# A hybrid decoder layer on one core: smaller descriptor scratch, final gain loaded ahead, twelve diagonals and one dot column per slot, the last two row gathers and the last norm in halves

## The chip, the cores and the metric

The kernel runs on one core of one Trainium2 chip. The metric is the device time of one execution in microseconds (us). Times quoted from the trace are microseconds from the start of the profiled span.

## What is computed

One decoder layer over 256 tokens of width 1024, in float32: a mixer with two groups of attention heads, a cross-attention to 256 memory tokens, a PEER feed-forward part, and a final RMSNorm. The change touches the last two:

```python
def peer_ffn(h, w_query, sub_keys_1, sub_keys_2, expert_down, expert_up):
    # per token: 8 heads, each picks the 16 best of 128 x 128 experts
    ...
    eidx = jnp.take_along_axis(cand_idx, pos, axis=-1)
    g = jax.nn.softmax(top_s, axis=-1)
    u = expert_down[eidx]
    a = jax.nn.gelu(jnp.einsum('cd,chkd->chk', xc, u), approximate=False)
    vv = expert_up[eidx]
    return jnp.einsum('chk,chkd->cd', g * a, vv)
...
x = x + peer_ffn(rmsnorm(x, norm_ffn), ...)
return rmsnorm(x, norm_final)     # y * rsqrt(mean(y*y) + eps) * norm_final
```

For each token 8 x 16 = 128 experts are picked. Of each one a row of `expert_down` (1024 numbers) is dotted with the normed token, and a row of `expert_up` is added to the token's sum with the weight gate x gelu(dot).

## The kernel before, in words

The 256 tokens are two tiles of 128 tokens, one token per partition. Up to about 237 us the kernel does the mixer, the memory attention of tile 0 and the first head's key search. From there to the end it runs the PEER part: 256 **slots**, numbered n, 128 for each tile (16 for each of 8 heads H). The two tables lie side by side in DRAM, so that one gathered row is 8 KB (down half, then up half). One slot is:

- POOL (loop in the `gpsimd` block, L597): an indirect DMA fetches for each of the 128 tokens its row into a buffer of [128, 2048], 1 MB in all. It first waits until TensorE has used up the buffer's former content (`up_used`). The buffers form a ring of 6, later 8, 10 and, from slot 100, 12 (`RINGS`).
- DVE (`dot`, L1169): multiplies the down half with the normed token and sums into a column of `dots`, when the rows are there (`row_in`).
- ACT (`weight`, L770, L774, L779): gelu of the dot, times the gate, and a 128 x 128 diagonal matrix of it in `diag`.
- PE (`up`, L1480): diagonal x up half, two matmuls of 512 columns, accumulated in PSUM (`y` for tile 0, `v_bank` for tile 1). `h_psum` and `a_bank` hold the normed tokens.

`NS = 6` columns of `dots` and diagonals exist. So DVE also waits in slot n for the gelu of slot n-6, and ACT waits before the diagonal for PE's slot n-6. Between the slots, at places written out by hand (`slots`, `top_at`), stand the rest of tile 1's layer and the key search of the next heads on DVE (`top_part`). That search ends in the expert numbers (`IDX`, parts "ones", "picks", "experts") for which POOL waits at each head. The part "ones" and the part "picks" are two instructions of 128 x 256 each.

The final norm (`root` on ACT, `finish` on DVE) is done for tile 0 after slot 134 and for tile 1 after the last slot. ACT squares and sums the row from PSUM and takes the root, DVE takes the reciprocal and multiplies row, root and gain in one instruction (L1181), SP writes 512 KB to DRAM (L565). The gain `gfin` (a row of 4 KB, broadcast to 128 partitions, 512 KB) lies in a weight slot that `w_xo` uses before. So SP issues its load (L561) only after a wait on tile 1's product with `w_xo`.

SP issues the loads of weights in program order (L504, L558, L561). The program's descriptor scratch for POOL's DMAs has its default size.

Of the kernel before, what the change touches and what calls it, by code (L numbers as in the profile page):

```python
# [17 lines left out]
P = 128  # L18
D = 1024
SEQ = 256  # L20
T = SEQ // P
# [14 lines left out]
NS = 6  # L36
# [27 lines left out]
def hybrid_layer(nc, A, out, bias_scratch):  # L64
# [200 lines left out]
    with ctx:  # L265
# [78 lines left out]
        GATE = sb("gates", [P, 3, PK])  # L344

        dots = sb("dots", [P, NS])
# [3 lines left out]
        sums_r = diag_r.rearrange("p (a b) x -> p a (b x)", a=3)  # L350
        small, small_r = diag[0:NH, :, :].rearrange("p (a b) x -> p a (b x)", a=3), sums_r[0:NH, :, :]
# [23 lines left out]
        gfin = W[:, wslot("w_xo", 0), 0:D]  # L375
# [59 lines left out]
        out_ready, out_done = sem("out_ready"), sem("out_done")  # L435

# [21 lines left out]
        roots += [("root_y", 0, 0), ("root_y", 1, 0)]  # L458
# [9 lines left out]
        def col(name, t, i):  # L468
            return {"root_m": i, "root_h": 2 + t, "o_root": 4 + 2 * t + i, "root_x": 8 + 2 * t,
                    "root_p": 9 + 2 * t, "root_y": 12 + t}[name]  # L470
# [3 lines left out]
        ROWS += [W[:, wslot("w_xo", 1), 2 * D * i:2 * D * (i + 1)] for i in range(2)]  # L474

# [16 lines left out]
        def _(sp):  # L492
# [70 lines left out]
            for t in range(T):  # L563
                sp.wait_ge(out_ready, t + 1)
                sp.dma_start(out[0, t * P:(t + 1) * P, :], YS[t]).then_inc(out_done, 16)  # L565
# [4 lines left out]
        def _(pool):  # L570
# [13 lines left out]
            pool.memset(diag_r[:, :, :].bitcast(f32), 0.0).then_inc(sums_zero, 1)  # L584
            pool.iota(iota16[:], [[1, PK]], base=0, channel_multiplier=0,
                      allow_small_or_imprecise_dtypes=True).then_inc(io_ready, 1)
            for n in range(T * SPT):
# [7 lines left out]
                elif buffer(n) in FREED_BY:  # L595
                    pool.wait_ge(*full(FREED_BY[buffer(n)]))
                pool.indirect_dma_start(ROWS[buffer(n)], None, expert_rows,  # L597
                                        bass.IndirectOffsetOnAxis(ap=IDX[:, H % 3, k:k + 1], axis=0))\
                    .then_inc(row_in[buffer(n)], 16)
# [3 lines left out]
        def _(act):  # L603
# [162 lines left out]
            def weight(n):  # L766
# [3 lines left out]
                nc.scalar.activation(gel[:, i:i + 1], dots[:, i:i + 1], ACT.Gelu, scale=rms("root_p", n // SPT)).then_inc(gelu_done, 1)  # L770
# [25 lines left out]
            act.wait_ge(up_used, T * SPT)  # L796
            root(("root_y", 1, 0), YP[1][:, :], HTpage[1], D)
# [3 lines left out]
        def _(dve):  # L801
# [284 lines left out]
            def top_part(part, H):  # L1086
# [48 lines left out]
                elif part == "ones":  # L1135
                    after(top_mark["pairs"])
                    for s in range(2):
                        top_mark[part] = t_mark(nc.vector.tensor_tensor(
                            hot[:, s, :, :], pabf[:, s, :].unsqueeze(2).broadcast_to([P, PK, PK]),
                            iota16[:, :].unsqueeze(1).broadcast_to([P, PK, PK]), ALU.is_equal))  # L1140
                elif part == "picks":
                    after(top_mark["ones"])
                    for s in range(2):
                        top_mark[part] = t_mark(nc.vector.tensor_tensor(
                            hot[:, s, :, :], hot[:, s, :, :],
                            kf[:, s, :].unsqueeze(1).broadcast_to([P, PK, PK]), ALU.mult))
                elif part == "experts":
                    after(top_mark["picks"])
                    after(t_mark(nc.vector.tensor_reduce(picked[:, :, :], hot[:, :, :, :], AX.X, ALU.add)))
                    nc.vector.scalar_tensor_tensor(out=IDX[:, H3, :], in0=picked[:, 0, :], scalar=float(NKEY),  # L1150
# [12 lines left out]
            def dot(n):  # L1163

                i, rows = n % NS, ROWS[buffer(n)][:, 0:D]
# [23 lines left out]
            for n in range(T * SPT):  # L1189
# [14 lines left out]
                if n == SPT + NS:  # L1204
                    finish(0, YP[0][:, :])
            finish(1, YP[1][:, :])


        assert buffer(SIDE_END) == 0 and RING % NS == 0
# [331 lines left out]
```

## Time and profile before

| what | value |
|---|---|
| time, median of 3 runs (lowest, highest) | 906.3 us (903.89, 907.79) |
| time of the profiled execution | 904.22 us |
| its span, first to last instruction | 902.4 us |
| PE, DVE, ACT, POOL busy | 796.0, 561.9, 433.6, 242.8 us |
| moved by POOL's queue (q0) | 268.45 MB in 36,864 packets |
| mean granted TensorE clock | 0.985 |

The profiled execution's time is its span and 1.8 us that lie around it. Busy times add up what each engine does, whatever the others do meanwhile. What sets the end is read from the chain of waits and from the stretches in which one resource never pauses.

### The profile page before, as it was taken

The numbers are of one execution on the slowest core, as the hardware profiler recorded it, in microseconds if no ns is written. First come the engines' busy times: TensorE is split into PE (matmuls) and PEld (weight loads), VectorE is DVE, ScalarE is ACT, GpSimd is POOL, SyncE is SP. The second block draws the span as 40 slices with busy tenths as digits, with TensorE's granted clock in tenths as the row PEclk, the third lists the DMA queues.
The fourth block names the chain that finished last, engine by engine and source line by source line (L and its number), as shares of the span: only waits on it lengthen the run. The fifth ranks groups of instructions, "written<-read, shape, count | busy, mean of one in ns | idle before, by whom it ended". The sixth has DMA issues, their size and how long they took to land.

```text
span 902.4 us, 10121 instructions
## 1 busy us (share of the span) xinstructions
PE 796.0 (88%) x3195; PEld 450.2 (50%) x3195; DVE 561.9 (62%) x1396; ACT 433.6 (48%) x1078; POOL 242.8 (27%) x268
## 2 busy tenths in 40 slices
PE   7999999999999999889898997989787877788776
PEld 7999987785455455444343552444232222222221
DVE  5555344123778767777776748787676766666443
ACT  5435555333245554667444445535355353535333
POOL 0000000000143333433343341624333333343310
PEclk9999999999999999999999899999999999999999
DMA  9898532072399999999999999999999999999993
GB/s 332 235 293 288 195 133 94 1 280 93 142 405 421 391 423 421 415 422 421 422 420 421 421 421 410 401 416 423 421 422 421 422 422 421 422 422 421 422 420 133
DMA packets 63317, 314.24 MB, mean 348 GB/s; under 512 B 7899, under 2 KB 12068, under 8 KB 30500
## 3 DMA queue, kind: packets, MB, share of 16 engines
q0 software_dynamic: 36864, 268.45, 71.9%
q1 hardware_dynamic: 25308, 43.61, 13.8%
q10 hardware_dynamic: 1096, 1.59, 1.2%
q8 instruction: 23, 0.38, 0.2%
q14 instruction: 26, 0.21, 0.1%
HBM read 311.01 MB, written 2.62 MB: 348 GB/s over the span
## 4 chain that ended last, share of the span: by engine, by line
PE 42%; DMA 38%; ACT 9%; issue 5%; DVE 5%; POOL 1%; POOLq 0%; ACTq 0%
DMA weights<-in_expert_rows,expert_idx 24%; PE y L1480 10%; DMA qkvb<-in_expert_rows,expert_idx 7%; PE v_bank L1480 7%; DMA mem_k<-in_expert_rows,expert_idx 6%; PE v_bank L1235 4%; PE a_bank L1245 4%; PE h_psum L1235 4%; PE v_bank L1245 3%; PE a_bank L1235 3%; PE h_psum L1245 3%; ACT diag L779 1%; ACT L770 1%; ACT L762 1%; ACT spare_r L676 1%
## 5 line engine op out<-in xcount | busy, mean ns | idle before, releaser
L597 POOL DMA_INDIRECT weights<-in_expert_rows,expert_idx x172 | 161.4, 939 | 260.7 <-PE y L1480 118.1
L770 ACT ACTIVATE gelu<-dots,stat 128x1 f32<-128x1 f32 x256 | 75.3, 294 | 307.0 <-DVE dots L1169 300.6
L1480 PE MATMUL v_bank<-weights,diag 128*128 128x512 f32 x344 | 169.9, 623 | 39.8 <-ACT diag L779 39.8
L1480 PE MATMUL y<-weights,diag 128*128 128x512 f32 x344 | 161.7, 606 | 17.7 <-ACT diag L779 17.5
L1169 DVE CUSTOM_DVE_ANT_0 weights<-a_bank,weights 128x1024 f32<-128x1024 f32 x86 | 105.3, 1224 | 74.9 <-DMA weights<-in_expert_rows,expert_idx 74.8
L1169 DVE CUSTOM_DVE_ANT_0 weights<-h_psum,weights 128x1024 f32<-128x1024 f32 x86 | 105.1, 1223 | 54.7 <-DMA weights<-in_expert_rows,expert_idx 52.6
L597 POOL DMA_INDIRECT qkvb<-in_expert_rows,expert_idx x54 | 51.0, 944 | 316.6 <-DVE expert_idx L1026 234.6
L1480 PEld LDWEIGHTS v_bank<-weights,diag 128*128 128x128 f32 x344 | 61.1, 193 | 144.7 <-ACT diag L779 94.0
L1480 PEld LDWEIGHTS y<-weights,diag 128*128 128x128 f32 x344 | 62.4, 191 | 98.2 <-issue 56.9
L779 ACT ACTIVATE diag<-ident,wgt 128x128 f32<-128x128 f32 x256 | 102.8, 402 | 8.4
L774 ACT ACTIVATE wgt<-gelu,gates 128x1 f32<-128x1 f32 x256 | 75.4, 295 | 8.3
L1480 PE MATMUL y<-qkvb,diag 128*128 128x512 f32 x136 | 66.5, 617 | 7.6 <-ACT diag L779 7.6
L889 DVE TENSOR_TENSOR weights_r<-weights,spare_r 128x2048 fp32r<-128x2048 f32 x19 | 43.5, 2291 | 36.9 <-ACT spare_r L676 36.9
L1169 DVE CUSTOM_DVE_ANT_0 qkvb<-h_psum,qkvb 128x1024 f32<-128x1024 f32 x34 | 41.6, 1223 | 22.1 <-DMA qkvb<-in_expert_rows,expert_idx 21.9
L1480 PE MATMUL v_bank<-qkvb,diag 128*128 128x512 f32 x80 | 40.4, 630 | 11.5 <-ACT diag L779 11.5
L676 ACT CAST spare_r<-weights 128x2048 fp32r<-128x2048 f32 x19 | 36.0, 1897 | 19.1 <-PE v_bank L1245 14.6
L1480 PEld LDWEIGHTS y<-qkvb,diag 128*128 128x128 f32 x136 | 24.6, 194 | 39.6 <-issue 21.0
L1245 PE MATMUL h_psum<-weights_r 128*128 128x256 f32 x128 | 36.2, 282 | 0.0
L1169 DVE CUSTOM_DVE_ANT_0 qkvb<-a_bank,qkvb 128x1024 f32<-128x1024 f32 x20 | 24.5, 1225 | 15.5 <-DMA qkvb<-in_expert_rows,expert_idx 15.5
L1480 PEld LDWEIGHTS v_bank<-qkvb,diag 128*128 128x128 f32 x80 | 13.9, 191 | 36.3 <-ACT diag L779 25.8
L1235 PE MATMUL v_bank<-weights,scaled_gffn 128*128 128x512 f32 x64 | 29.2, 595 | 0.6 <-issue 0.6
L1480 PE MATMUL v_bank<-mem_v,diag 128*128 128x512 f32 x44 | 21.7, 616 | 6.2 <-ACT diag L779 6.2
(288 smaller groups left out, 1281.7 us busy)
## 6 DMA issues: line engine op xcount, KB each, us to landing
weights<-in_w_in SPq DMA_DIRECT2D x5, 2048.0 KB, 32.3
weights<-in_w_xk SPq DMA_DIRECT2D x2, 2048.0 KB, 16.6
weights<-in_w_xv SPq DMA_DIRECT2D x2, 2048.0 KB, 10.7
weights<-in_w_out SPq DMA_DIRECT2D x2, 2048.0 KB, 8.8
weights<-in_w_xq SPq DMA_DIRECT2D x2, 2048.0 KB, 7.9
weights<-in_w_xo SPq DMA_DIRECT2D x2, 2048.0 KB, 11.1
weights<-in_expert_rows,expert_idx POOLq DMA_INDIRECT x172
weights<-in_w_in SPq DMA_DIRECT2D x2, 1024.0 KB, 8.5
```

The costliest lines, as they stand in the source:

```text
L597: pool.indirect_dma_start(ROWS[buffer(n)], None, expert_rows, bass.IndirectOffsetOnAxis(ap=IDX[:, H % 3, k:k + 1], axis=0))\
L676: act.copy(WH_r[t % 2], half_block(t, W)).then_inc(high_ready, 1)
L762: nc.scalar.activation(texp[:], tv[:], ACT.Exp, bias=tneg[:, 0:1], scale=rms("root_p", H // PH), accum_out=tsum[:, 0:1])\
L770: nc.scalar.activation(gel[:, i:i + 1], dots[:, i:i + 1], ACT.Gelu, scale=rms("root_p", n // SPT)).then_inc(gelu_done, 1)
L774: nc.scalar.activation(wgt[:, i:i + 1], gel[:, i:i + 1], ACT.Copy, scale=GATE[:, H % 3, k:k + 1])\
L779: nc.scalar.activation(diag[:, i, :], ident[:, :], ACT.Copy, scale=wgt[:, i:i + 1])\
L889: nc.vector.tensor_tensor(half_block(t, W_r), half_block(t, W), WH_r[t % 2].bitcast(f32), ALU.subtract).then_inc(low_ready, 1)
L1169: nc.vector.tensor_tensor_reduce(out=rows, in0=HP[n // SPT][:, :], in1=rows, scale=1.0, scalar=0.0, op0=ALU.mult, op1=ALU.add, accum_out=d ...
L1235: ins = nc.tensor.matmul(bank[:, lo:lo + n], lhs(k), rhs(k), start=(k == 0), stop=(k == chunks - 1))
L1245: ins = nc.tensor.matmul(bank[:, lo:lo + n], a(k), b(k), start=(k == 0 and p == 0), stop=(k == KC - 1 and p == 2))
L1480: ins = nc.tensor.matmul(YP[t][:, b * BLK:(b + 1) * BLK], diag[:, i, :], ROWS[r][:, D + b * BLK:D + (b + 1) * BLK], start=False, stop=last)
```

## The change

Six things are changed.

1. The descriptor scratch is given as 4,096 bytes a partition in place of the default.
2. `gfin` gets a tile of its own, and SP issues its load right behind the last weight load, with no wait.
3. `dots` has a column for each of the 256 slots, `gel`, `wgt` and `diag` have twelve. DVE's wait for the gelu of slot n-6 and ACT's wait for PE's slot n-6 are gone, with no new one in their place.
4. "ones" and "picks" are one instruction of 128 x 512 each.
5. The last two slots (254, 255) are gathered as half rows, in the order down 254, down 255, up 254, up 255, of 512 KB each. The table is seen as rows of 4 KB for this; DVE computes the half rows' numbers (`last_idx`) with the last head's expert numbers.
6. Slot 255 has no diagonal and no matmul. DVE adds up half x weight to PE's sum in two halves of 512 columns. ACT squares each half, DVE multiplies each by the gain meanwhile, and the row is scaled by the root's reciprocal, half on ACT and half on DVE. PE's matmuls of slot 254 report each half.

```diff
-NS = 6
+NS = 12
+DMA_SCRATCH = 4096
...
-        dots = sb("dots", [P, NS])
+        dots = sb("dots", [P, T * SPT])
...
-        gfin = W[:, wslot("w_xo", 0), 0:D]
+        gfin = sb("gfin", [P, D])[:, :]
...
-            sp.wait_ge(v_full, VN[("xo", 1, 0)] + 1)
             sp.dma_start(gfin, A["norm_final"].rearrange("(a d) -> a d", a=1).broadcast_to([P, D]))\
...
+                if n < LAST - 1:
...
+                else:
+                    i = n - (LAST - 1)
+                    pool.indirect_dma_start(ROWS[buffer(n)][:, 0:D], None, half_rows,
+                                            bass.IndirectOffsetOnAxis(ap=last_idx[:, i:i + 1], axis=0))\
+                        .then_inc(row_in[buffer(n)], 16)
+            for i in range(2):
+                pool.indirect_dma_start(ROWS[buffer(LAST - 1 + i)][:, D:2 * D], None, half_rows,
+                                        bass.IndirectOffsetOnAxis(ap=last_idx[:, 2 + i:3 + i], axis=0)).then_inc(up_in[i], 16)
...
+                if n == LAST:
+                    return
                 act.wait_ge(w_done, n + 1)
-                if n >= NS:
-                    act.wait_ge(up_used, n - NS + 1)
...
             nc.scalar.activation(stat[:, 15:16], eps[:, 0:1], ACT.Sqrt)
-            act.wait_ge(up_used, T * SPT)
-            root(("root_y", 1, 0), YP[1][:, :], HTpage[1], D)
+            for b in range(2):
+                act.wait_ge(last_sum, b + 1)
+                nc.scalar.activation(hp[:, last_half[b]], YS[1][:, last_half[b]], ACT.Square, accum_out=last_sq[b])\
+                    .then_inc(last_square, 1)
+            act.wait_ge(last_square, 2)
+            act.wait_ge(last_eps, 1)
+            nc.scalar.activation(last_sq[1], last_sq[1], ACT.Sqrt, bias=last_sq[0], scale=1.0 / D).then_inc(sq_done, 1)
+            act.wait_ge(last_root, 1)
+            act.wait_ge(last_gain, 1)
+            nc.scalar.activation(YS[1][:, last_half[0]], last_gained[:, last_half[0]], ACT.Copy, scale=last_sq[1])\
+                .then_inc(last_ready, 1)
...
-                if n >= NS:
-                    dve.wait_ge(gelu_done, n - NS + 1)
...
+            def finish_last():
+                i = LAST % NS
+                dve.wait_ge(w_done, LAST + 1)
+                dve.wait_ge(up_in[1], 16)
+                for b in range(2):
+                    dve.wait_ge(half_used, b + 1)
+                    nc.vector.scalar_tensor_tensor(out=YS[1][:, last_half[b]],
+                                                   in0=ROWS[buffer(LAST)][:, D + b * BLK:D + (b + 1) * BLK],
+                                                   scalar=wgt[:, i:i + 1], in1=YP[1][:, last_half[b]],
+                                                   op0=ALU.mult, op1=ALU.add).then_inc(last_sum, 1)
...
+            pe.wait_ge(diag_done, LAST)
+            pe.wait_ge(up_in[0], 16)
+            for b in range(2):
+                nc.tensor.matmul(YP[1][:, b * BLK:(b + 1) * BLK], diag[:, (LAST - 1) % NS, :],
+                                 ROWS[buffer(LAST - 1)][:, D + b * BLK:D + (b + 1) * BLK], start=False, stop=True)\
+                    .then_inc(half_used, 1)
...
-    nc = bacc.Bacc("TRN2", target_bir_lowering=False, num_devices=1)
+    nc = bacc.Bacc("TRN2", target_bir_lowering=False, num_devices=1, dynamic_dma_scratch_size=DMA_SCRATCH)
```

DVE at the end of the program, before (`ISA ...dots` is the dot, the `ISA dots` row behind it reads its sum):

```order
L1169 ISA mem_v,dots<-a_bank,mem_v 128x1024 [waits gelu_done,row_in9]
L1169 ISA dots 128x1
L1169 ISA weights,dots<-a_bank,weights 128x1024 [waits gelu_done,row_in10]
L1169 ISA dots 128x1
L1169 ISA weights,dots<-a_bank,weights 128x1024 [waits gelu_done,row_in11]
L1169 ISA dots 128x1
L820 RECIPROCAL stat<-stat 128x1 [waits sq_done]
L1181 SCALAR_TENSOR_TENSOR x_and_h<-v_bank,stat,weights 128x1024 [waits ld_gfin,dve_ch]
```

The same place with the change:

```order
L1204 ISA weights,dots<-a_bank,weights 128x1024 [waits row_in11]
L1204 ISA dots 128x1
L1224 SCALAR_TENSOR_TENSOR x_and_h<-weights,wgt,v_bank 128x512 [waits half_used,up_in1,w_done]
L1224 SCALAR_TENSOR_TENSOR x_and_h<-weights,wgt,v_bank 128x512 [waits half_used]
L1229 TENSOR_TENSOR x_and_h<-x_and_h,gfin 128x512 [waits last_sum]
L1232 TENSOR_SCALAR stat<-stat 128x1 [waits last_square]
L1233 TENSOR_TENSOR x_and_h<-x_and_h,gfin 128x512
L1236 RECIPROCAL stat<-stat 128x1 [waits sq_done]
L1239 TENSOR_SCALAR x_and_h<-x_and_h,stat 128x512 [waits last_gain,last_root]
```

Two instructions behind the last dot have become seven, of half the width.

DVE inside the slots, where a head's key search ends, before:

```order
L1138 TENSOR_TENSOR one_hot<-pos_ab_f,iota 128x256 [waits top_ch]
L1138 TENSOR_TENSOR one_hot<-pos_ab_f,iota 128x256
L1169 ISA weights,dots<-a_bank,weights 128x1024 [waits gelu_done,row_in11]
L1169 ISA dots 128x1
L1144 TENSOR_TENSOR one_hot<-one_hot,key_idx_f 128x256 [waits top_ch]
L1144 TENSOR_TENSOR one_hot<-one_hot,key_idx_f 128x256
L1169 ISA qkvb,dots<-a_bank,qkvb 128x1024 [waits gelu_done,row_in0]
```

And with the change:

```order
L1168 TENSOR_TENSOR one_hot<-pos_ab_f,iota 128x512 [waits top_ch]
L1204 ISA weights,dots<-a_bank,weights 128x1024 [waits row_in11]
L1204 ISA dots 128x1
L1173 TENSOR_TENSOR one_hot<-one_hot,key_idx_f 128x512 [waits top_ch]
L1204 ISA qkvb,dots<-a_bank,qkvb 128x1024 [waits row_in0]
```

Each dot now waits for one semaphore in place of two. An instruction that waits for a second semaphore has an instruction that only waits in front of it, which these rows don't show. In the program as built, DVE has 1,569 instructions before, 297 of which only wait, and 1,299 with the change, 49 of which only wait. ACT has 1,350 (333 only wait) before, and 1,103 (85) with the change. PE, POOL and SP differ by two at most.

## Rows read from the trace of the kernel before

**Rows 1.** Page, part 2 (GB/s in 40 slices of 22.6 us) and part 3 (queue: packets, MB, share)
```profile
GB/s 332 235 293 288 195 133 94 1 280 93 142 405 421 391 423 421 415 422 421 422 420 421 421 421 410 401 416 423 421 422 421 422 422 421 422 422 421 422 420 133
...
q0 software_dynamic: 36864, 268.45, 71.9%
```

**Rows 2.** Waits from 250 to 902 us: who waited for whom, total us, times, longest
```profile
DVE weights L1169 <- DMA weights<-in_expert_rows,expert_idx: 127.5, 145, 2.0
```

**Rows 3.** Timeline of DVE: the dot of slot 225 (start us, us, engine, line, operation)
```profile
817.50 1.23 DVE L1169 CUSTOM_DVE_ANT_0 weights<-a_bank,weights 128x1024 f32<-128x1024 f32 x1 [1.67 <-DMA weights<-in_expert_rows,expert_idx]
```

**Rows 4.** Busy time in a stretch: PE, PEld, DVE, ACT, POOL, clock, DMA share, GB/s
```profile
885.00:892.00 7.00, 5.55 (x13) 1.81 (x11) 3.33 (x6) 2.97 (x9) 0.00 (x0) 1.00 0.12 50
```

**Rows 5.** Timeline from the dot of slot 255 to the last store, 892 to 900 us
```profile
892.01 1.22 DVE L1169 CUSTOM_DVE_ANT_0 weights<-a_bank,weights 128x1024 f32<-128x1024 f32 x1 [1.23 <-DMA weights<-in_expert_rows,expert_idx]
...
893.93 0.40 ACT L779 ACTIVATE diag<-ident,wgt 128x128 f32<-128x128 f32 x1
894.35 1.28 ACT L795 ACT_TABLE_LOAD   x1
...
894.38 1.98 PE L1480 MATMUL v_bank<-weights,diag 128*128 128x512 f32 x4 [0.47 <-ACT diag L779]
...
895.64 0.20 ACT L795 ACTIVATE stat<-eps 128x1 f32<-128x1 f32 x1
896.40 1.02 ACT L614 ACTIVATE x_and_h<-v_bank 128x1024 f32<-128x1024 f32 x1 [0.56 <-PE v_bank L1480]
...
897.55 0.29 ACT L627 ACTIVATE stat<-stat,eps 128x1 f32<-128x1 f32 x1
897.88 0.16 DVE L820 RECIPROCAL stat<-stat 128x1 f32<-128x1 f32 x1 [4.64 <-ACT stat L627]
898.08 1.28 DVE L1181 SCALAR_TENSOR_TENSOR x_and_h<-v_bank,stat,weights 128x1024 f32<-128x1024 f32 x1
899.39 0.34 SPq L565 DMA_DIRECT2D out<-x_and_h  x1
```

**Rows 6.** Groups by form: tiles, shapes, count, busy us, mean ns, idle before
```profile
L875 DVE TENSOR_TENSOR x_and_h_r<-x_and_h,scaled_gffn_r 128x512 fp32r<-128x512 f32 x4 | 2.6, 683 | 0.0
L614 ACT ACTIVATE qkvb<-x_and_h 128x512 f32<-128x512 f32 x4 | 2.5, 626 | 6.5 <-DVE x_and_h L951 6.5
L959 DVE TENSOR_SCALAR x_and_h<-x_and_h,stat 128x512 f32<-128x512 f32 x4 | 1.9, 486 | 0.1
```

**Rows 7.** Timeline of POOL: the gathers of slots 113 and 255
```profile
512.25 0.94 POOL L597 DMA_INDIRECT qkvb<-in_expert_rows,expert_idx  x1 [0.53 <-issue]
...
866.92 0.94 POOL L597 DMA_INDIRECT weights<-in_expert_rows,expert_idx  x1 [1.55 <-PE v_bank L1480]
```

**Rows 8.** Timeline: the load of the gain on SP, and the dots of slots 88, 90, 91
```profile
465.30 0.34 SPq L561 DMA_DIRECT2D weights<-in_norm_final  x1
...
468.03 1.22 DVE L1169 CUSTOM_DVE_ANT_0 mem_k<-h_psum,mem_k 128x1024 f32<-128x1024 f32 x1 [0.72 <-DMA mem_k<-in_expert_rows,expert_idx]
...
474.27 1.22 DVE L1169 CUSTOM_DVE_ANT_0 qkvb<-h_psum,qkvb 128x1024 f32<-128x1024 f32 x1 [1.34 <-DMA qkvb<-in_expert_rows,expert_idx]
477.70 1.22 DVE L1169 CUSTOM_DVE_ANT_0 qkvb<-h_psum,qkvb 128x1024 f32<-128x1024 f32 x1 [1.67 <-DMA qkvb<-in_expert_rows,expert_idx]
```

**Rows 9.** DMA queues from 468 to 474 us: packets, MB, share of 16 engines
```profile
q1 hardware_dynamic: 143, 0.52, 21.8%
```

**Rows 10.** The page's group of the diagonals: busy us, mean ns, idle before
```profile
L779 ACT ACTIVATE diag<-ident,wgt 128x128 f32<-128x128 f32 x256 | 102.8, 402 | 8.4
```

**Rows 11.** Timeline: the dots of slots 177 and 178
```profile
695.41 1.23 DVE L1169 CUSTOM_DVE_ANT_0 weights<-a_bank,weights 128x1024 f32<-128x1024 f32 x1 [0.73 <-DMA weights<-in_expert_rows,expert_idx]
698.79 1.23 DVE L1169 CUSTOM_DVE_ANT_0 weights<-a_bank,weights 128x1024 f32<-128x1024 f32 x1 [1.77 <-DMA weights<-in_expert_rows,expert_idx]
```

**Rows 12.** DMA queues from 696 to 698 us
```profile
q14 instruction: 1, 0.01, 1.0%
```

**Rows 13.** Timeline: the gather of slot 25 on POOL and its dot on DVE
```profile
301.82 0.98 POOL L597 DMA_INDIRECT qkvb<-in_expert_rows,expert_idx  x1 [2.57 <-PE y L1480]
...
309.57 1.23 DVE L1169 CUSTOM_DVE_ANT_0 qkvb<-h_psum,qkvb 128x1024 f32<-128x1024 f32 x1 [2.37 <-DMA qkvb<-in_expert_rows,expert_idx]
```

More of the change, by code:

```diff
@@ L435, in hybrid_layer @@
         out_ready, out_done = sem("out_ready"), sem("out_done")
+        up_in, half_used = [sem(f"up_in{i}") for i in range(2)], sem("half_used")
+        last_sum, last_square, last_eps, last_gain = sem("last_sum"), sem("last_square"), sem("last_eps"), sem("last_gain")
+        last_root, last_ready = sem("last_root"), sem("last_ready")
         def bank_of(key):
@@ L474, in hybrid_layer @@
         ROWS += [W[:, wslot("w_xo", 1), 2 * D * i:2 * D * (i + 1)] for i in range(2)]
+        LAST = T * SPT - 1
+        last_sq = [stat[:, 13 + b:14 + b] for b in range(2)]
+        last_half = [slice(b * BLK, (b + 1) * BLK) for b in range(2)]
+        last_gained = HTpage[1]
         def rms(name, t):
@@ L559, in _ @@
                              [:, :, b * BLK:(b + 1) * BLK]).then_inc(ld_query[b], 16)
-            sp.wait_ge(v_full, VN[("xo", 1, 0)] + 1)
             sp.dma_start(gfin, A["norm_final"].rearrange("(a d) -> a d", a=1).broadcast_to([P, D]))\
                 .then_inc(ld_gfin, 16)
-            for t in range(T):
-                sp.wait_ge(out_ready, t + 1)
-                sp.dma_start(out[0, t * P:(t + 1) * P, :], YS[t]).then_inc(out_done, 16)
+            sp.wait_ge(out_ready, 1)
+            sp.dma_start(out[0, 0:P, :], YS[0]).then_inc(out_done, 16)
+            sp.wait_ge(last_ready, 2)
+            sp.dma_start(out[0, P:2 * P, :], YS[1]).then_inc(out_done, 16)
             sp.wait_ge(out_done, 16 * T)
@@ L1136, in top_part @@
                     after(top_mark["pairs"])
[L1137 to L1140, printed above, removed]
+                    top_mark[part] = t_mark(nc.vector.tensor_tensor(
+                        hot[:, :, :, :], pabf[:, :, :].unsqueeze(3).broadcast_to([P, 2, PK, PK]),
+                        iota16[:, :].unsqueeze(1).unsqueeze(1).broadcast_to([P, 2, PK, PK]), ALU.is_equal))
                 elif part == "picks":
                     after(top_mark["ones"])
[L1143 to L1146, printed above, removed]
+                    top_mark[part] = t_mark(nc.vector.tensor_tensor(
+                        hot[:, :, :, :], hot[:, :, :, :],
+                        kf[:, :, :].unsqueeze(2).broadcast_to([P, 2, PK, PK]), ALU.mult))
                 elif part == "experts":
@@ L1149, in top_part @@
                     after(t_mark(nc.vector.tensor_reduce(picked[:, :, :], hot[:, :, :, :], AX.X, ALU.add)))
+                    if H == T * PH - 1:
+                        after(t_mark(nc.vector.scalar_tensor_tensor(
+                            out=last_expert[:, :], in0=picked[:, 0, PK - 2:PK], scalar=float(NKEY),
+                            in1=picked[:, 1, PK - 2:PK], op0=ALU.mult, op1=ALU.add)))
+                        for half in range(2):
+                            t_mark(nc.vector.tensor_scalar(last_idx[:, 2 * half:2 * half + 2], last_expert[:, :], 2.0,
+                                                           float(half), ALU.mult, ALU.add))
                     nc.vector.scalar_tensor_tensor(out=IDX[:, H3, :], in0=picked[:, 0, :], scalar=float(NKEY),
@@ L1203, in _ @@
                     top_part(part, H)
[L1204 to L1206 removed]
+                if n == SPT + 6:
+                    finish_first()
+            finish_last()
         assert buffer(SIDE_END) == 0 and RING % NS == 0
```

45 lines of the change are left out of this document (30 added, 15 removed).

## The prediction

> **What bounds the kernel now.** I read the page first. Its GB/s slices stand at 420 or near it from slice 12 to 39, and POOL's queue has moved 268.45 MB [rows 1]. So the slot part is one long gather. The waits say the same: DVE stood 127.5 us in 145 waits for rows of the weight buffers alone [rows 2], and no engine is waited for on the way to a landing. The timeline gives the beat. The dot of slot 225 starts at 817.50 [rows 3], that of slot 255 at 892.01 [rows 5], both straight behind their landing: 74.51 us for 30 slots, 2.484 us each.
>
> The beat is not the mean engine's. From 885 to 892 us the DMA engines move only 50 GB/s [rows 4], 350 KB in all, while slots 253 to 255 still land one beat apart. So most DMA engines have finished, and one or two last ones (64 KB per slot in 2.484 us is 26.4 GB/s each) set every landing. What is put into or taken out of their work after slot 25 therefore shows at the end one to one. A pause of POOL that does not outlast the backlog shows nowhere.
>
> Behind the last landing comes a chain of its own [rows 5]: dot 892.01, diagonal 893.93, matmuls 894.38 to 896.36, square 896.40, root 897.55, reciprocal 897.88, product 898.08, store issued 899.39, end of the span 902.4. That is 10.4 us, 7.4 of them up to the store's issue. The change can work in two places, the DMA engines' queue and this chain.
>
> **The end of the program.** Let L be the landing of the last rows, 892.01 now. With halves in the order down, down, up, up, each half beat is 1.24 us, so the down half of slot 255 lands at L-2.48, the up half of 254 at L-1.24. I walk the engines.
> - ACT: the diagonal starts 1.92 us behind the start of a dot [rows 5]. For 254 it ends at L-3.73+1.92+0.40 = L-1.4. For 255 the weight is ready near L-0.6; then the table load (1.28) and the dummy root run from about L-0.5 to L+1.0, where the table load now lies under the matmuls.
> - PE: 1.98 us for both halves of a slot [rows 5], 0.99 each. It starts at L-1.24 and gives the halves at L-0.25 and L+0.75.
> - DVE: a 128x512 operation of two tensors takes 0.68 us [rows 6]. First sum L to L+0.7, second L+0.8 to L+1.5, first product with the gain to L+2.2, the small eps step, second product to L+3.0.
> - ACT: square of 512 columns 0.63 us [rows 6] and some 0.15 for the read of its sum: L+1.0 to L+1.8, then to L+2.55. Root (0.29) to L+2.9, covered by DVE's second product.
> - Reciprocal (0.16) to L+3.2, then a half on DVE (0.49) and one on ACT (about 0.6, by the square's row) side by side: L+3.9.
>
> The store is issued at L+3.9 in place of L+7.4, and what follows it stays 3.0 us. **Gain 3.5 us.** DVE's order is the limit. If the handshakes cost 0.1 us more at each of eight steps it is 2.7; if the squares start earlier than I have them, up to 4.2.
>
> The two extra gathers of POOL cost nothing: slot 255's gather is issued at 866.92 [rows 7] and lands 25.1 us later, ten beats of backlog against two more issues of 1.24 us. No other queue stands behind them. DVE gets three small instructions for the halves' numbers in the last key search, some 0.6 us of a DVE that waits over 1 us per beat, long before the end.
>
> What a half gather costs the DMA engines I take from the only 512 KB transfer with 4 KB rows amid the gathers, the gain's (next part): 1.27 us, against 1.24 for half a beat. So four halves cost 4 x 1.27 in place of 2 x 2.484, 0.1 us more. The upper bound is 0.6 us, if 4 KB rows ran as the load in the next part at its worst.
>
> The Trainium skill speaks against this step ("DMA: Bandwidth & Descriptors", "Anatomy of one DMA"): it gives each transfer of POOL's path about 2.0 us fixed and bytes over 436 GB/s, and its rule is to batch to 1 MiB or more. As an estimate from that page, two more transfers would cost 4 us if they ran one behind the other. The trace shows a 1 MB slot each 2.484 us, less than the 4.4 us of that formula, so the fixed part overlaps here.
>
> **The gain's load.** SP issues it at 465.30, in the middle of the gathers [rows 8], and 0.52 MB pass on its queue from 468 to 474 us [rows 9]. From slot 88 to slot 90 the dots take 6.24 us for two beats (4.97): 1.27 us late, a half beat's worth. With the change the load is issued right behind the query load at about 212 us, where the slices show 93 and 142 GB/s [rows 1], before the first gather. The same bytes go where nothing waits. **Gain 1.27 us**; bounds 0 (if the beat were PE's there) and 2.2 (if the next late slot were its doing too). What comes after is one unbroken backlog, so nothing takes it back.
>
> **The waits.** ACT stood idle 8.4 us before all 256 diagonals [rows 10], 0.033 each, the bare handshake. DVE's waits in the dots are for rows. Neither of the two removed waits ever held anything, and twelve diagonals in place of six free nothing. The one-instruction "ones" and "picks" save about 0.15 us per head on DVE, which waits for rows anyway. As waits, all of it is worth zero.
>
> As instructions it may not be. Slot 178's dot starts 3.38 us behind slot 177's [rows 11], 0.9 over the beat, and 2 us earlier the instruction queue moved a packet [rows 12]. I found that step of 0.9 us before slots 91, 118, 154, 178, 201 and 225, each with a packet of that queue in the 2 to 4 us before; other packets of it had no effect. Between the four last of these the built program has 115, 114 and 114 DVE instructions, and 13 more by the rows that a search splits into two: 128 each time. So DVE's own instruction stream is fetched over one of the late DMA engines, 128 instructions at a time. Slot 25 to 255 has 582.4 us [rows 13, 5], 571.3 by the beat. Of the 11.1 over it 1.27 is the gain's load, as much again tile 0's store, and the rest is nine steps of 0.93. With the change DVE has 1,012 instructions there against 1,263, so 7.9 fetches in place of 9.9. **Gain 1.9 us**, bounds 0 (the steps have another cause) and 2.8 (one more fetch falls out).
>
> **Sum.** 3.5 + 1.27 + 1.9 - 0.1 = 6.6 us. The profiled execution goes from 904.2 to 897.6, its span from 902.4 to 895.8. The median before is 906.3, 2.1 above the profiled one, so against it I expect 899.7.
>
> **Rivals.**
> - *The instruction steps stay.* The steps of 0.9 us come from something periodic and not from DVE's fetches. For it: 8 KB at 26.4 GB/s are 0.3 us, a third of the step. Against it: the count of 128 holds three times. Then 904.2 - 4.7, or 901.6 against the median, about at the edge of what counts as faster.
> - *The tail gives less.* The handshakes between three engines, or the halves landing later, leave 1 to 1.5 us of 3.5, and one fetch falls badly. Sum 3 us: 903.3.
> - *The scratch throttles POOL (slower).* POOL must find room in the scratch for its descriptors. Each slot has 144 packets (36,864 by 256 [rows 1]), 9 per DMA engine, and a smaller scratch is reused more often. If POOL let its transfers drain at such a point, the next slot would land no sooner than 7.75 us after its issue, as slot 25 did with a near empty queue (301.82 to 309.57 [rows 13]), 5.3 us beyond the beat. The trace doesn't tell how often that would be. One drain in 32 slots is eight, 42 us: 942 against the median. Two drains already eat the forecast's gain, and it begins where fewer than about three slots can be in flight. Against it: POOL's gathers take 0.94 us at slot 113 as at slot 255, with 0.53 us idle before the one and a wait for PE before the other [rows 7], so the scratch of before shows no such point in mid stream.
>
> By the Trainium skill ("SBUF — State Buffer", "SBUF size: 192, 224, or 256?" and "DMA: Bandwidth & Descriptors", "The descriptor swizzle") the default scratch is 16 KiB and a 1 MiB transfer takes 9 descriptors per engine and side, at 16 B each. As an estimate 4 KiB then hold 28 transfers against 10 in flight, and no throttle follows. No run so far shows the smaller size.
>
> **How the numbers follow.** A measurement of this kernel can tell about 0.5% from no change, 4.5 us, so "faster" is below 901.8 us. The forecast has 0.50, the staying steps 0.24, the small tail 0.18, the throttle 0.05; 0.03 is for what I don't see. The forecast with its bounds is faster nearly always, the second case about half the time, the third rarely: faster 0.64, within 0.5% 0.29, slower 0.07. The range takes the sum's own ends (2.5 to 9 us off the median) and the 2 us by which single executions differ: 895.5 to 904.8. It leaves out the throttle.
>
> **What would show it.** The store's issue 3.9 us behind the last landing, and 6.9 from there to the end of the span (a longer chain: the tail rival). The gain's load before 225 us, and no late slots at 89 and 90. The 0.9 us steps 28 to 30 slots apart in the last hundred slots, in place of 24 (if still 24: the first rival). The beat unchanged at 2.484 us; a longer beat, or POOL idle with free buffers and no engine to wait for, would be the throttle and would prove me wrong. DVE and ACT busy times should hardly differ.

## The result and the profile after

| | before | changed |
|---|---|---|
| time, median (lowest, highest), 7 runs each | 905.09 us (903.89, 908.65) | 897.94 us (897.27, 901.68) |
| ratio, 95% interval | | 0.9918 [0.9903, 0.9933] |
| profiled execution, its span | 904.22, 902.4 us | 897.27, 895.5 us |

The kernel is 0.8% faster: 7.1 us by the medians, 6.9 by the spans of the two profiled executions. The forecast was 899.7 (897.6 for a profiled execution), range 895.5 to 904.8.

The page of the changed kernel, parts 2 and 3:

```profile
GB/s 333 233 287 303 178 152 94 1 282 118 112 407 422 393 424 420 411 421 421 422 420 423 421 421 422 412 422 422 420 422 422 422 421 422 422 421 421 422 422 201
...
q0 software_dynamic: 37152, 268.45, 72.4%
```

The bytes of POOL's queue are the same, with 288 packets more (two transfers of 144) than in [rows 1]. The slices stand at the same 420.

The timeline of the changed kernel answers to [rows 8]. The gain's load is now issued at 212 us, and the dots of slots 88 to 91 stand one beat apart:

```profile
212.29 0.58 SPq L573 DMA_DIRECT2D gfin<-in_norm_final  x1
...
467.14 1.22 DVE L1204 CUSTOM_DVE_ANT_0 mem_k<-h_psum,mem_k 128x1024 f32<-128x1024 f32 x1 [0.72 <-DMA mem_k<-in_expert_rows,expert_idx]
469.61 1.22 DVE L1204 CUSTOM_DVE_ANT_0 mem_v<-h_psum,mem_v 128x1024 f32<-128x1024 f32 x1
472.10 1.23 DVE L1204 CUSTOM_DVE_ANT_0 qkvb<-h_psum,qkvb 128x1024 f32<-128x1024 f32 x1 [0.86 <-DMA qkvb<-in_expert_rows,expert_idx]
474.58 1.23 DVE L1204 CUSTOM_DVE_ANT_0 qkvb<-h_psum,qkvb 128x1024 f32<-128x1024 f32 x1 [0.71 <-DMA qkvb<-in_expert_rows,expert_idx]
```

Two beats take 4.96 us, where they took 6.24.

A late slot is one whose dot starts 0.9 us or more over the beat behind the dot before it, as slot 178 does in [rows 11]. Before, they were 91, 118, 154, 178, 201 and 225. Now they are 109, 160, 190 and 220, two fewer, and the last three stand thirty apart. (Slots 101 and 135 are late in every kernel, by 2.8 and 4.5 us. They are left out here.) Here are slots 189 and 190 of the changed kernel:

```profile
722.32 1.23 DVE L1204 CUSTOM_DVE_ANT_0 weights<-a_bank,weights 128x1024 f32<-128x1024 f32 x1 [0.91 <-DMA weights<-in_expert_rows,expert_idx]
...
725.78 1.23 DVE L1204 CUSTOM_DVE_ANT_0 weights<-a_bank,weights 128x1024 f32<-128x1024 f32 x1 [1.82 <-DMA weights<-in_expert_rows,expert_idx]
```

3.46 us, 0.98 over the beat.

The end of the changed kernel, from the dot of slot 253 on, answers to [rows 5]:

```profile
883.35 1.22 DVE L1204 CUSTOM_DVE_ANT_0 mem_v<-a_bank,mem_v 128x1024 f32<-128x1024 f32 x1 [1.23 <-DMA mem_v<-in_expert_rows,expert_idx]
...
884.59 1.22 DVE L1204 CUSTOM_DVE_ANT_0 weights<-a_bank,weights 128x1024 f32<-128x1024 f32 x1
...
885.72 1.98 PE L1538 MATMUL v_bank<-mem_v,diag 128*128 128x512 f32 x4 [0.47 <-ACT diag L801]
...
885.84 1.23 DVE L1204 CUSTOM_DVE_ANT_0 weights<-a_bank,weights 128x1024 f32<-128x1024 f32 x1
...
887.54 1.88 PE L1577 MATMUL v_bank<-weights,diag 128*128 128x512 f32 x4
...
887.74 1.28 ACT L817 ACT_TABLE_LOAD   x1
...
888.71 1.50 DVE L1224 SCALAR_TENSOR_TENSOR x_and_h<-weights,wgt,v_bank 128x512 f32<-128x512 f32 x2 [1.64 <-PE v_bank L1577]
...
889.49 0.60 ACT L820 ACTIVATE h_psum<-x_and_h 128x512 f32<-128x512 f32 x1 [0.25 <-DVE x_and_h L1224]
...
890.24 0.69 DVE L1229 TENSOR_TENSOR x_and_h<-x_and_h,gfin 128x512 f32<-128x512 f32 x1
...
890.91 0.68 DVE L1233 TENSOR_TENSOR x_and_h<-x_and_h,gfin 128x512 f32<-128x512 f32 x1
891.09 0.29 ACT L824 ACTIVATE stat<-stat 128x1 f32<-128x1 f32 x1
891.51 0.15 DVE L1236 RECIPROCAL stat<-stat 128x1 f32<-128x1 f32 x1
891.70 0.72 ACT L827 ACTIVATE x_and_h<-x_and_h,stat 128x512 f32<-128x512 f32 x1 [0.32 <-DVE stat L1236]
891.70 0.48 DVE L1239 TENSOR_SCALAR x_and_h<-x_and_h,stat 128x512 f32<-128x512 f32 x1
892.45 0.34 SPq L578 DMA_DIRECT2D out<-x_and_h  x1
```

The down halves of slots 254 and 255 follow slot 253 at half beats (1.24, 1.25 us). The table load lies under the matmuls and the root under DVE's second product. From the dot of slot 253 to the store's issue it is now 9.10 us; before it was 12.30 (887.09 to 899.39). To the end of the span it is 12.1, before 15.3. So the end is 3.2 us shorter.

So the two profiles differ in three stretches. Up to the dot of slot 60: 397.5 and 397.0 us, 0.5 less. From slot 60 to slot 253, 193 beats of 2.4835 us: 10.25 and 7.01 us over the beat, 3.24 less. From there to the end 3.2 less. Together 6.9.

### The profile page after: what moved, and what is told of

It reads as the page before. It is cut to its first block, busy times and chain, and to the rows that moved or that the text cites. A ratio compares the mean times of both kernels' runs of the same rounds, so it can differ in the third digit from the quotient of the medians.

```text
span 895.5 us, 9600 instructions
## 1 busy us (share of the span) xinstructions
PE 788.4 (88%) x3191; PEld 447.6 (50%) x3191; DVE 561.7 (63%) x1374; ACT 433.9 (48%) x1080; POOL 247.5 (28%) x270
## 4 chain that ended last, share of the span: by engine, by line
DMA 40%; PE 40%; ACT 8%; DVE 8%; issue 3%; POOL 1%; ACTq 0%; POOLq 0%; DVEq 0%
DMA mem_v<-in_expert_rows,expert_idx 14%; DMA mem_k<-in_expert_rows,expert_idx 11%; PE y L1538 10%; DMA qkvb<-in_expert_rows,expert_idx 8%; DMA weights<-in_expert_rows,expert_idx 7%; PE v_bank L1293 4%; PE v_bank L1538 4%; PE a_bank L1303 4%; PE h_psum L1293 4%; PE v_bank L1303 3%; PE a_bank L1293 3%; PE h_psum L1303 3%; ACT diag L801 1%; DVE weights L1204 1%; DVE qkvb L1204 1%
## 5 line engine op out<-in xcount | busy, mean ns | idle before, releaser
L1538 PE MATMUL v_bank<-weights,diag 128*128 128x512 f32 x336 | 163.7, 617 | 37.4 <-ACT diag L801 37.4
L1538 PE MATMUL y<-weights,diag 128*128 128x512 f32 x344 | 158.9, 599 | 16.6 <-ACT diag L801 16.5
L1538 PEld LDWEIGHTS v_bank<-weights,diag 128*128 128x128 f32 x336 | 59.1, 191 | 138.1 <-ACT diag L801 89.7
```

Of the source, the lines that this page charges most:

```text
L1538: ins = nc.tensor.matmul(YP[t][:, b * BLK:(b + 1) * BLK], diag[:, i, :], ROWS[r][:, D + b * BLK:D + (b + 1) * BLK], start=False, stop=last)
```

## The experiments

All kernels but only_scratch are the changed kernel with something put back, added or moved, or as it is (after_again). Three numbers of each come from its trace. The span is known to 0.1 us, so the last column is good to 0.05. The ratios come from five to twelve executions each, beside the kernel before on the same chip.

| kernel | ratio to before, 95% | span | dot of slot 60 | over the beat, 60 to 253 | slot 253 to end |
|---|---|---|---|---|---|
| before | | 902.4 | 397.5 | 10.25 | 15.31 |
| changed | 0.9918 [0.9903, 0.9933] | 895.5 | 397.0 | 7.01 | 12.15 |
| dve_wait | 0.9952 [0.9934, 0.9971] | 898.3 | 397.9 | 8.96 | 12.08 |
| dve_two | 0.9941 [0.9917, 0.9965] | 898.7 | 398.5 | 8.76 | 12.11 |
| dve_three | 0.998 [0.9965, 0.9996] | 904.6 | 402.8 | 10.39 | 12.11 |
| act_wait | 0.9927 [0.9905, 0.9949] | 896.7 | 398.0 | 7.27 | 12.13 |
| gain_late | 0.9949 [0.9929, 0.9969] | 898.2 | 398.3 | 8.41 | 12.15 |
| whole_old_norm | 0.9975 [0.9955, 0.9995] | 900.9 | 399.3 | 6.89 | 15.36 |
| halves_old_norm | 0.9951 [0.9937, 0.9966] | 898.3 | 398.1 | 7.12 | 13.81 |
| store_late | 0.994 [0.9915, 0.9964] | 897.8 | 401.1 | 5.27 | 12.09 |
| store_late_again | 0.9905 [0.989, 0.9919] | 895.5 | 398.0 | 6.05 | 12.16 |
| only_scratch | 1.0002 [0.9986, 1.0018] | 903.2 | 398.9 | 9.62 | 15.31 |
| scratch_1k | 0.9924 [0.991, 0.9938] | 898.9 | 400.6 | 6.83 | 12.13 |
| after_again | 0.9921 [0.9907, 0.9936] | 900.1 | 402.2 | 6.48 | 12.07 |

The ratios of kernels that ran on different chips can't be compared as closely as the stretches. One kernel, store_late and store_late_again, has 0.994 on one chip and 0.9905 on another, 3.2 us apart at 905. The changed kernel has its ratio from the first measurement and from a chip on which only_scratch, scratch_1k and store_late_again ran as well. The other seven kernels with something put back are slower than it by their ratios (0.8 us for act_wait, 2.8 for gain_late, 3.1 for dve_wait, 5.2 for whole_old_norm, 5.6 for dve_three) by more than their last two columns say (0.26, 1.4, 1.95, 3.1, 3.4). In their traces all of them reach slot 60 later than the first profile of the changed kernel, which was early (see the part on the scatter). The prices below are those of the stretches.

### Does the number of DVE's instructions set the late slots?

The first kernel puts DVE's wait back:

```diff
                 dve.wait_ge(row_in[buffer(n)], 16 * (len(users(n)) + 1))
+                if n >= 6:
+                    dve.wait_ge(gelu_done, n - 6 + 1)
```

> The changed kernel with DVE's wait for the gelu of six slots back put into each dot again; the wait is always met, so it holds nothing, but it adds 250 DVE instructions that only wait. Theory (DVE's own instruction fetch costs one step of 0.93 us in the landings each 128 instructions): the last steps stand 24 slots apart in place of 30, about 2 steps more from slot 25 on, 1.9 us slower than the changed kernel, 899.2 in the profile. Rival (something periodic): the steps stay 30 slots apart, no difference.

The late slots are 93, 120, 158, 184, 206 and 231, two more than in the changed kernel. The last four stand 24 apart on average, and the stretch is 1.95 us longer, two steps. Slots 205 and 206 of this kernel:

```profile
764.92 1.22 DVE L1206 CUSTOM_DVE_ANT_0 mem_v<-a_bank,mem_v 128x1024 f32<-128x1024 f32 x1 [0.91 <-DMA mem_v<-in_expert_rows,expert_idx]
768.36 1.23 DVE L1206 CUSTOM_DVE_ANT_0 weights<-a_bank,weights 128x1024 f32<-128x1024 f32 x1 [1.79 <-DMA weights<-in_expert_rows,expert_idx]
```

The second puts ACT's wait back:

```diff
                 act.wait_ge(w_done, n + 1)
+                if n >= NS:
+                    act.wait_ge(up_used, n - NS + 1)
                 nc.scalar.activation(diag[:, i, :], ident[:, :], ACT.Copy, scale=wgt[:, i:i + 1])\
```

> The changed kernel with ACT's wait for PE of twelve slots back put before each diagonal again; always met, 243 ACT instructions more that only wait. Theory: the steps of 0.93 us stay at slots 160, 190 and 220 and the time stays within 0.5 us, since only DVE's fetches cost. Rival (any engine's instruction traffic costs): 2 steps more, 1.9 us slower.

The late slots stay at 109, 160, 190 and 220; the stretch is 0.26 us longer, within what two runs of one kernel differ by (7.01 and 6.48). Slots 189 and 190:

```profile
723.43 1.23 DVE L1206 CUSTOM_DVE_ANT_0 weights<-a_bank,weights 128x1024 f32<-128x1024 f32 x1 [0.92 <-DMA weights<-in_expert_rows,expert_idx]
...
726.87 1.23 DVE L1206 CUSTOM_DVE_ANT_0 weights<-a_bank,weights 128x1024 f32<-128x1024 f32 x1 [1.80 <-DMA weights<-in_expert_rows,expert_idx]
```

Two kernels with more waits in the dots followed:

> The changed kernel with two waits put into each dot again, both always met, 500 DVE instructions more. Theory: steps 19 to 20 slots apart, nearly 4 steps more than the changed kernel, 3.6 us slower, 900.9 in the profile. Rival: steps 30 slots apart, no difference.

The forecast was wrong, since the kernel isn't what it took it for: two waits share one instruction, so it has one instruction more than dve_wait in all, 1,549 against 1,548. The late slots are 158, 183, 206 and 231 again, 1.75 us more than the changed kernel. So twice the waits in the same number of instructions change nothing: it is the instructions that count. With three waits

```diff
+                if n >= 6:
+                    dve.wait_ge(gelu_done, n - 6 + 1)
+                    dve.wait_ge(w_done, n - 6 + 1)
+                    dve.wait_ge(diag_done, n - 6 + 1)
```

> The changed kernel with three waits put into each dot again, all always met. The built program has 499 DVE instructions more than the changed one (two waits share one instruction, so the kernel with two waits had only as many as the one with one). Theory: steps of 0.95 us 19 slots apart in the last hundred slots, 3 steps more from slot 60 on than the changed kernel, 3 us slower. Rival (the waits themselves, not their number, move the steps): as with one wait, 24 slots apart, 2 us slower.

DVE has 1,798 instructions, the late slots from 150 on are 154, 174, 196, 216 and 238, 21 apart where 19 were expected, and the stretch is 3.4 us over the changed kernel's. What the instruction queue moved from 236 to 880 us tells the engines apart. Row q14 of the DMA view of the kernel before, the changed one, dve_wait, dve_three and act_wait, in this order:

```profile
q14 instruction: 22, 0.18, 0.1%
```
```profile
q14 instruction: 18, 0.15, 0.1%
```
```profile
q14 instruction: 20, 0.16, 0.1%
```
```profile
q14 instruction: 22, 0.18, 0.1%
```
```profile
q14 instruction: 20, 0.16, 0.1%
```

ACT's wait and DVE's wait each bring two packets back, but only DVE's packets bring late slots. So the rival of something periodic falls, and so does "any instruction traffic". What is shown: from about slot 90 on, each 128 DVE instructions cost the landings 0.95 us, waits that are always met included, and the same packets for ACT cost nothing that can be told.

The trace's semaphore records say why the two engines differ. A gather counts its semaphore up sixteen times, and its slot can start with the last of these. From slot 150 on, the sixteenth comes 1.0 us or more behind the fifteenth in every trace that was kept, and 2.6 us in the last landing of the changed kernel. Taking each increment for the end of one part of the gather, one part in sixteen sets the beat. In act_wait a packet of the instruction queue moves at 724.48. For slot 190 the first fifteen increments then come 2.48 to 2.50 us behind those of slot 189, and only the sixteenth is late (3.44). Another packet moves at 703.98. For slot 183 only the fifteenth is late (3.17), and the sixteenth comes on the beat, 1.8 us behind it. It is the same in all fourteen traces: from slot 155 to slot 245 each late slot has its sixteenth increment late by 0.9 to 1.0 us, and the other packets delay earlier increments by 0.3 to 0.9, which nothing waits for. In act_wait and in the kernel before, these others stand 126 to 134 of ACT's recorded instructions apart, about 30 slots. In the changed kernel they stand 129 apart on average, 34 to 44 slots. So they are ACT's. DVE's packets delay the part that comes last, and ACT's one that has time.

### The gain's load

```diff
+            sp.wait_ge(v_full, VN[("xo", 1, 0)] + 1)
             sp.dma_start(gfin, A["norm_final"].rearrange("(a d) -> a d", a=1).broadcast_to([P, D]))\
```

> The changed kernel with the gain's load put back behind the wait on tile 1's product with w_xo, amid the gathers; it keeps its own tile. Theory: 0.52 MB come back into the late DMA engine's work, dots of slots 88 to 91 late by 1.27 us in all, 1.3 us slower. Rival (a beat set by PE there, or the load's 4 KB rows at half rate): 0, or 2.2 us.

Slots 88 to 91 of this kernel:

```profile
469.04 1.23 DVE L1205 CUSTOM_DVE_ANT_0 mem_k<-h_psum,mem_k 128x1024 f32<-128x1024 f32 x1 [0.72 <-DMA mem_k<-in_expert_rows,expert_idx]
472.14 1.23 DVE L1205 CUSTOM_DVE_ANT_0 mem_v<-h_psum,mem_v 128x1024 f32<-128x1024 f32 x1 [0.75 <-DMA mem_v<-in_expert_rows,expert_idx]
475.25 1.23 DVE L1205 CUSTOM_DVE_ANT_0 qkvb<-h_psum,qkvb 128x1024 f32<-128x1024 f32 x1 [1.48 <-DMA qkvb<-in_expert_rows,expert_idx]
477.74 1.23 DVE L1205 CUSTOM_DVE_ANT_0 qkvb<-h_psum,qkvb 128x1024 f32<-128x1024 f32 x1 [0.72 <-DMA qkvb<-in_expert_rows,expert_idx]
```

6.21 us for two beats, 1.25 us late, and the next slot on the beat. In the kernel before, slot 91 was late by 0.95 as well; here it is not. That confirms that this third late slot was an instruction step and not the load. The stretch is 1.4 us longer.

### The end in two parts

Two kernels undo the end. The first gathers the last two rows whole, sends slot 255 through diagonal and PE, and squares, roots and multiplies the row in one piece. The second keeps the half gathers and undoes the rest; PE waits for each up half:

```diff
-            for b in range(2):
-                act.wait_ge(last_sum, b + 1)
-                nc.scalar.activation(hp[:, last_half[b]], YS[1][:, last_half[b]], ACT.Square, accum_out=last_sq[b])\
+            act.wait_ge(up_used, T * SPT)
+            nc.scalar.activation(HTpage[1], YP[1][:, :], ACT.Square, accum_out=last_sq[0]).then_inc(last_square, 1)
...
-                nc.vector.tensor_scalar(YS[1][:, last_half[1]], last_gained[:, last_half[1]], last_sq[1], None, ALU.mult)\
+                nc.vector.scalar_tensor_tensor(out=YS[1], in0=YP[1][:, :], scalar=last_sq[0], in1=gfin,
+                                               op0=ALU.mult, op1=ALU.mult).then_inc(last_ready, 1)
...
+                if n >= LAST - 1:
+                    pe.wait_ge(up_in[n - (LAST - 1)], 16)
+                flat_up(n)
```

> The changed kernel with the last two slots gathered as whole rows, a diagonal and matmuls for slot 255 again, and the last norm in one piece as before. Theory: the chain behind the last landing is 10.4 us again in place of 7.2, 3.2 us slower than the changed kernel, the landings unchanged. Rival (the halves also cost or give something in the DMA engines): a difference other than 3.2 us, seen in the landing of the last rows.

> The changed kernel with the half gathers kept, but slot 255 through diagonal and PE, and the norm in one piece. Theory: the last landing is slot 255's up half, and only its two matmuls (1.98 us) and the norm (4.4 us up to the store's issue) stand behind it; the diagonal is ready before. So some 1.5 us slower than the changed kernel and 1.7 faster than with whole rows. Rival (the gain is all in the norm's halves): as slow as with whole rows.

With whole rows and the old norm, slot 253 to the end takes 15.3 us again, 3.2 more than the changed kernel, and the landings before it are as in the changed kernel. The dot of slot 253 and the last store of whole_old_norm are 12.31 us apart, in place of 9.10:

```profile
885.54 1.22 DVE L1186 CUSTOM_DVE_ANT_0 mem_v<-a_bank,mem_v 128x1024 f32<-128x1024 f32 x1 [1.24 <-DMA mem_v<-in_expert_rows,expert_idx]
...
897.85 0.34 SPq L578 DMA_DIRECT2D out<-x_and_h  x1
```

With the halves kept they are 10.82 apart (884.49 to 895.31). So the half gathers alone give 1.5 us and the sum on DVE with the norm in halves 1.7. The end of halves_old_norm:

```profile
888.69 3.60 PE L1512 MATMUL v_bank<-weights,diag 128*128 128x512 f32 x8
...
892.32 1.02 ACT L817 ACTIVATE x_and_h<-v_bank 128x1024 f32<-128x1024 f32 x1 [1.52 <-PE v_bank L1512]
...
894.00 1.28 DVE L1213 SCALAR_TENSOR_TENSOR x_and_h<-v_bank,stat,gfin 128x1024 f32<-128x1024 f32 x1
895.31 0.34 SPq L578 DMA_DIRECT2D out<-x_and_h  x1
```

PE does both last slots in one go from 888.69 to 892.29. It starts 1.7 us behind the dot of slot 255 (886.97), and the last landing is 2.5 behind that dot, so PE is within the first slot's matmuls when it comes and has all of slot 255's still to do.

### The descriptor scratch

> The kernel before with the descriptor scratch of 4,096 bytes and nothing else. Theory: the scratch neither costs nor gives time, ratio 1.000 within 0.2%, 10.3 us over the beat from slot 60 to 253 as before. Rival (the scratch throttles, or its place in memory helps the late engine): a changed beat or pauses of POOL with buffers free.

> The changed kernel with 1,024 bytes of descriptor scratch. Theory: if a transfer takes nine descriptors of 16 bytes per engine, only seven transfers fit, so POOL pauses for room in place of buffers and about seven slots are in flight in place of ten (17 us from gather to dot in place of 25); the late engine never runs dry and the time stays within 1 us. Rival (POOL waits for an empty queue when it needs room): slots land in bursts with gaps of 5 us, 40 us slower or more.

The kernel before with nothing but `dynamic_dma_scratch_size=4096` takes the same time (1.0002). It has the late slots 91, 118, 154, 178, 201 and 225 as before, and slots 89 and 90 by the load. The small scratch gives room and no time: as the program is built, the changed kernel's tiles don't fit beside a scratch of the default size.

With 1,024 bytes POOL's waits change, from 250 to 890 us:

```profile
POOL weights L611 <- issue: 124.6, 85, 2.5
...
POOL weights L611 <- PE v_bank L1538: 26.3, 17, 1.6
```

In the changed kernel the same two groups read:

```profile
POOL weights L611 <- PE v_bank L1538: 102.0, 72, 3.2
...
POOL weights L611 <- issue: 4.6, 15, 0.3
```

POOL now waits for nothing that the profile shows. That it is room in the scratch is inferred, since only the scratch was changed. The gather of slot 253 and its dot, timelines of POOL and DVE:

```profile
869.87 0.94 POOL L611 DMA_INDIRECT mem_v<-in_expert_rows,expert_idx  x1 [1.54 <-issue]
...
886.77 1.22 DVE L1204 CUSTOM_DVE_ANT_0 mem_v<-a_bank,mem_v 128x1024 f32<-128x1024 f32 x1 [1.24 <-DMA mem_v<-in_expert_rows,expert_idx]
```

16.9 us in place of 25.2, which is seven slots in flight in place of ten, as was expected. The beat stays, and the ratio (0.9924) is the changed kernel's. No wait is longer than 2.5 us, so POOL waits for room one slot at a time and doesn't drain its queue.

### A version that takes more out of the late engine's work

```diff
             sp.wait_ge(out_ready, 1)
+            sp.wait_ge(up_in[1], 16)
             sp.dma_start(out[0, 0:P, :], YS[0]).then_inc(out_done, 16)
```

> The changed kernel with tile 0's store (512 KB) held back until the last half rows have landed; its data is ready since slot 135. Theory: the store leaves the late DMA engine's work amid the gathers and runs while the DMA engines idle in the last chain (4 us from landing to the second store's issue), 1.25 us faster than the changed kernel. Rival: the two stores collide at the end and the second one lands later, no gain or 1 us slower.

> The kernel with tile 0's store held back, a second time, beside the changed kernel. Theory: the stretch from slot 60 on is 1.3 to 1.7 us shorter again and the median is 1.3 us below the changed kernel's; what was lost before slot 60 in its first run was scatter. Rival: the loss before slot 60 comes back, and with it a median no better than the changed kernel's.

The stores of store_late_again:

```profile
888.34 0.36 SPq L577 DMA_DIRECT2D out<-x_and_h  x1
892.45 0.34 SPq L579 DMA_DIRECT2D out<-x_and_h  x1
```

The mechanism is there in both runs. From slot 134 to slot 146, over which tile 0's store passed, all twelve kernels that keep it there are 2.14 to 2.19 us over the beat, and these two 0.97 and 0.95: 1.2 us gone, with 12.1 us from slot 253 to the end as before. In the time it is less clear. Beside the changed kernel on one chip the median is 1.4 us lower (897.27 against 898.68), as forecast, and each of its five executions (896.66 to 897.56) is faster than each of the changed kernel's six (897.64 to 901.98). But the closest two are 0.1 us apart, the intervals of the ratios overlap (0.9905 and 0.9921), and its first run, on another chip with no changed kernel beside it, gave 0.994. By the trace it beats the changed kernel; by the times that rests on this one comparison.

### Scatter before slot 60

> The changed kernel itself, for a comparison on one chip with the next three. All theories: 0.992 of the kernel before. In the trace: steps at slots 160, 190, 220 again, and 7.0 us over the beat from slot 60 to slot 253; the slots up to 60 may differ by 2 to 4 us, as they did between the runs so far.

The time and the later stretches came again (ratio 0.9921, late slots 160, 190, 220), but the profiled execution took 900.1 us, 4.6 more: 5.2 more before slot 60, and 0.5 less behind it. Most of it has a visible cause. TensorE's busy time and granted clock from 54 to 60 us in after_again:

```profile
54.00:56.00 2.00, 0.17 (x1) 0.20 (x2) 1.69 (x1) 1.97 (x2) 0.00 (x0) 1.00 0.99 382
56.00:58.00 2.00, 2.00 (x16) 2.00 (x16) 1.55 (x1) 1.36 (x2) 0.00 (x0) 0.84 0.95 357
58.00:60.00 2.00, 2.00 (x11) 2.00 (x11) 1.87 (x2) 0.00 (x0) 0.00 (x0) 0.50 1.05 391
```

and in the first profile of the changed kernel from 8 to 12 us:

```profile
8.00:10.00 2.00, 1.62 (x8) 1.29 (x8) 1.55 (x4) 1.01 (x2) 0.00 (x0) 0.63 1.10 348
10.00:12.00 2.00, 1.99 (x10) 1.83 (x10) 1.47 (x3) 2.00 (x3) 0.00 (x0) 0.51 1.19 265
```

In both the clock falls to half, 1.2 of 2.4 GHz, for about 3.4 us. The fall at 8 to 12 us cost nothing: loads are still coming in there, and at 53.7 us PE is at the same matmul in both kernels. In after_again PE then stands idle for 1.84 us up to 55.83. It waits for DVE, DVE for ACT, and ACT for a load of `w_in`. From there it works on without a pause, and 3.4 us at half the clock cost it 1.7. The two add up to 3.5, and the first slot's dot starts at 248.5 in place of 244.9.

The other 1.7 us came between slots 0 and 60, where the first profile of the changed kernel is the fastest of all that were kept (152.1 us; the others take 152.6 to 155.8). store_late takes 155.8 there. Its windows of ten us from 340 to 360 us:

```profile
340.00:350.00 10.00, 8.06 (x28) 4.76 (x27) 7.54 (x18) 5.58 (x16) 2.26 (x3) 0.83 1.01 418
350.00:360.00 10.00, 10.00 (x46) 6.17 (x46) 6.05 (x21) 4.42 (x13) 4.68 (x5) 1.00 0.91 325
```

Here too PE pauses, its clock is at half for 3.4 us (from 343.8), and the DMA engines then move 325 GB/s from 350 to 360 us, where the changed kernel's move 420. dve_three has the same fall at 346.1. Behind it, from slot 40 to slot 48, these two take 22.6 and 22.4 us, the other twelve profiles 19.8 to 21.3, and none of these has a fall between 320 and 380 us. That the fall is the cause was not tested. The rest of the scatter stays unexplained. It is why single spans are no measure here and the stretches are.

## Why the prediction was right

The size, the sign and the three places hold. Point by point:

- **The gain's load**: forecast 1.27 us; 1.28 in the dots of slots 88 to 90, and 1.25 when put back. Right.
- **The instructions**: forecast 1.9 us, two fewer fetches, steps 28 to 30 slots apart. Measured: two late slots fewer, 30 apart, and 1.96 us for what is left of the stretch's 3.24 after the load. The step that I held weakest, that a wait that never waits costs time, was the one that the waits put back show best. "One or two" last DMA engines set each landing by the prediction; the sixteenth increments show that it is one part. They also show that ACT's packets delay another, which the prediction didn't ask about.
- **The end**: forecast 3.5 us less 0.1 for the half gathers, measured 3.2 from slot 253 on. One term was off, "PE starts at L-1.24". The landing is at 888.34, by the store that waits for it in store_late_again, whose last sum and last store start at the same hundredth as the changed kernel's, and PE starts at 887.54, L-0.8. It was still at slot 253's matmuls until 887.70, which I had not followed. So DVE's first sum starts 0.37 us behind the landing. The rest of DVE's and ACT's order came as worked out: the store is issued at L+4.1 in place of L+3.9, and what follows takes 3.0.
- **The halves' cost**: forecast 0.1 us. From the dot of slot 253 to the last landing it is 4.99 us (883.35 to 888.34), against 4.92 for two whole rows before. Right. With that the fixed cost for each transfer that the Trainium skill gives ("DMA: Bandwidth & Descriptors", "Anatomy of one DMA") shows nowhere in the landings.
- **The waits as waits, twelve diagonals, joined "ones" and "picks"**: forecast zero; DVE's and ACT's busy times differ by 0.2 and 0.3 us, and the beat is the same. Neither the twelve diagonals nor the joined parts were tried alone.
- **The scratch**: forecast no effect; 1.0002. The Trainium skill's numbers ("DMA: Bandwidth & Descriptors", "The descriptor swizzle"), nine descriptors for each engine, agree with seven slots in flight at 1,024 bytes (16.9 us by the beat are 6.8 slots).

One part of the measured gain is no merit of the change: the first profile of the changed kernel reached slot 60 earlier than any other run, 0.5 us before the kernel before, by luck as after_again shows. Without it the two profiles differ by 6.4 us, and the forecast was 6.6.

What stays open is why a packet of 8 KB, whose share of the queues' time is 0.3 us, delays the last part by 0.95, and why this part is late at all. No record here names the DMA engine of a packet or of an increment.

## What to carry to other kernels

In this kernel one stream of transfers keeps the DMA engines busy to the end. A constant of 512 KB amid it cost 1.3 us and an early store of the same size 1.2, half a beat each. The constant cost nothing where the engines idled. Look for such bytes where a stream like this sets the time. Follow the landings' beat and explain each slot that breaks it; that showed here two costs of 1 us that no group and no wait showed. And a wait that is always met isn't free here: as an instruction of its own in a long unrolled stream on DVE it is fetched too.

## What I had not expected

- About 250 DVE instructions that only wait cost 1.8 to 2.0 us of 900, and 499 of them 3.4 us, on an engine that stands idle over a third of the time. About as many on ACT cost nothing that can be told (0.26 us).
- One part in sixteen of each gather comes last, 1 us or more behind the other fifteen, and sets every landing late in the kernel. What delays only the others costs nothing.
- A scratch with room for seven transfers in place of ten changed neither the beat nor the time.
- The same kernel reaches slot 60 between 397.0 and 402.2 us.
